# Twenty ring rows, and dots that read the tokens from PSUM

## The reference, cut to what matters

```python
for l in range(DEPTH):                         # 2
    h = _rms(x, g_mix_norm[l])
    x = x + _mixer_block(h, ...)               # w_in (1024 -> 2816), four mixers, w_out
    h = _rms(x, g_ffn_norm[l])
    x = x + _peer(h, w_peer_q[l], peer_sub_keys[l], peer_u[l], peer_v[l])

# _peer, for each chunk of 128 tokens
q = (xc @ w_q).reshape(C, PEER_HEADS, 2, PEER_HALF)          # 8 heads
s = einsum('thpd,hpkd->thpk', q, sub_keys)                   # 128 keys twice
sv, si = top_k(s, 16); cand = all 16 x 16 sums of the two; top, pos = top_k(cand, 16)
eidx = index of the chosen pair (one of 16384); g = softmax(top)
a = einsum('thkd,td->thk', u_tab[eidx], xc)                  # a dot per token and chosen expert
w = g * gelu(a)
return einsum('thk,thkd->td', w, v_tab[eidx])                # weighted sum of the v rows
```

## Time and profile before

| | us |
|---|---|
| three executions | 3384.54, 3361.59, 3390.99 |
| median | 3384.54 |
| profiled execution, first to last instruction (span) | 3383.4 |
| PE busy | 2560.1 |
| DVE busy | 2327.2 |
| POOL busy | 2291.7 |
| ACT busy | 690.9 |
| mean of DMA over the span | 356 GB/s, 1205.57 MB |

### The profile page before, as it was taken

The page is one execution under the profiler, slowest core; times in us unless marked ns, Lnnn a source line. Parts: engine busy times, 40 slices in busy tenths (PEclk is TensorE's granted clock), DMA queues, the critical chain, the costliest instruction groups (busy, mean ns, idle before and its releaser), DMA issues.

```text
span 3383.4 us, 27538 instructions
## 1 busy us (share of the span) xinstructions
PE 2560.1 (76%) x7696; PEld 1422.5 (42%) x7696; DVE 2327.2 (69%) x5442; ACT 690.9 (20%) x1655; POOL 2291.7 (68%) x2052
## 2 busy tenths in 40 slices
PE   6568777986777778877787787987787778666667
PEld 5545344743443435533353443643354334222222
DVE  2495678568689875666668886666668888655554
ACT  2112212123311111112211221123322122101011
POOL 0156766566667676676776777677777777777776
PEclk9789888988888888998899998998899899888888
DMA  5489999998899999998999999999999999999998
GB/s 235 174 320 406 358 377 371 343 378 310 308 376 367 347 344 407 401 379 332 352 394 369 379 373 348 390 397 344 348 358 397 363 382 368 368 367 359 366 366 336
DMA packets 316375, 1205.57 MB, mean 356 GB/s; under 512 B 37184, under 2 KB 37440, under 8 KB 301248
## 3 DMA queue, kind: packets, MB, share of 16 engines
q0 software_dynamic: 294912, 1073.87, 83.9%
q1 hardware_dynamic: 21312, 129.94, 9.7%
HBM read 1201.57 MB, written 2.10 MB: 356 GB/s over the span
## 4 chain that ended last, share of the span: by engine, by line
PE 30%; POOL 22%; issue 18%; DVE 17%; DMA 7%; ACT 3%; another core or an unknown queue 2%; SPq 0%; DVEq 0%; ACTq 0%; POOLq 0%
POOL ring L479 22%; PE psY L815 15%; PE psP L694 8%; DMA ring<-in_v,idx 6%; DVE ring L1067 5%; PE psP L689 4%; DVE x L1076 1%; DMA ring<-in_u,idx 1%; DVE sc L860 1%; PE psT L675 1%; ACT diag L656 1%; DVE hot L1031 1%; DVE hot L1032 1%; DVE pick L1033 1%
## 5 line engine op out<-in xcount | busy, mean ns | idle before, releaser
L815 PE MATMUL psY<-ring,diag 128*128 128x512 f32 x3120 | 1689.6, 685 | 678.0 <-DMA ring<-in_v,idx 270.3
L479 POOL DMA_INDIRECT ring<-in_u,idx x1024 | 1148.1, 1121 | 588.1 <-issue 304.3
L1067 DVE CUSTOM_DVE_ANT_0 ring<-ring,htok 128x1024 f32<-128x1024 f32 x1024 | 1232.4, 1223 | 450.5 <-DMA ring<-in_u,idx 396.5
L479 POOL DMA_INDIRECT ring<-in_v,idx x1024 | 1143.3, 1117 | 490.2 <-issue 284.2
L815 PEld LDWEIGHTS psY<-ring,diag 128*128 128x128 f32 x3120 | 636.9, 216 | 1545.9 <-issue 1087.1
L656 ACT ACTIVATE diag<-cst,wgt 128x128 f32<-128x128 f32 x780 | 275.5, 393 | 480.8 <-PE psY L815 184.9
L1076 DVE SCALAR_TENSOR_TENSOR x<-ring,wgt,x 128x1024 f32<-128x1024 f32 x244 | 313.6, 1285 | 39.5 <-DMA ring<-in_v,idx 27.6
L694 PE MATMUL psP<-wr,hT 128*128 128x256 f32 x1392 | 312.7, 383 | 5.1 <-DMA wr<-in_w_out 3.0
L689 PE MATMUL psP<-hT,wr 128*128 128x256 f32 (+1 forms) x1664 | 314.8, 350 | 0.7 <-ACT hT L517 0.7
L689 PEld LDWEIGHTS psP<-hT,wr 128*128 128x128 f32 x1664 | 282.2, 200 | 49.7 <-issue 23.1
L694 PEld LDWEIGHTS psP<-wr,hT 128*128 128x128 f32 x1392 | 267.6, 193 | 65.4 <-issue 22.9
(11 more groups left out here) (125 smaller groups left out, 1652.3 us busy)
## 6 DMA issues: line engine op xcount, KB each, us to landing
wr<-in_w_in SPq DMA_DIRECT2D x44, 1024.0 KB
wr<-in_w_q SPq DMA_DIRECT2D x40, 1024.0 KB
wr<-in_w_out SPq DMA_DIRECT2D x19, 1024.0 KB
ring<-in_u,idx POOLq DMA_INDIRECT x1024
ring<-in_v,idx POOLq DMA_INDIRECT x1024
ring<-in_w_in SPq DMA_DIRECT2D x11, 1024.0 KB, 13.2
x<-in_x SPq DMA_DIRECT2D x4, 512.0 KB, 20.1
sub<-in_subkeys SPq DMA_DIRECT2D x2, 1024.0 KB
```

Source lines behind the costliest of these rows:

```text
L479: pool.indirect_dma_start(out=ring[:, q % NB], out_offset=None, in_=table, in_offset=bass.IndirectOffsetOnAxis(ap=idx[:, s % NS, n:n + 1], ...
L815: last = nc.tensor.matmul(psY[:, b * 512:(b + 1) * 512], diag[:, m % ND], r[:, b * 512:(b + 1) * 512], start=first, stop=final)
L1067: v.tensor_tensor_reduce(out=r, in0=r, in1=htok[:, s % NS], scale=1.0, scalar=0.0, op0=ALU.mult, op1=ALU.add, accum_out=adot[:, n:n + 1]). ...
```

## The change

- `NB` is 20. `W_EARLY` is 15 (input and output pieces of group 0), in ten places of two rows.
- `psH`, two banks, holds the normed tokens of the current chunk. `place_h` (ACT) copies them there from `htok` once the dots of the chunk before are done, ahead of the gelu of that chunk's last head; the dots read `psH` in place of `htok`. `adot` keeps two heads.
- To free two banks, `psP` and `psT` have one each. Odd pieces go to `psO`, even ones to `psP` (`piece_bank`). Of the wide transposes (hT1, qk, catT, hT2) the first four go to `psT`, the other four to `psS` (`batch_bank`, `wide_transposes`); dil T and conv use `psT` alone (`wait_pst`). `pso_free_for` and `pss_free` wait for the user before.
- To free memory for eight rows, buffers of the mixers and of the search are shared: `stick` lies in `tmq` (q and k pieces), `sub` in `prob` and `probT`, `gain_f` in `cat`, `qT` in `qdT`/`qsT`, `sc` in `later`, `sc2`, `cand` and `hot` in `fm`. New waits guard them (`tops_before`, `uses_before`).
- `sub` and `gain_f` are therefore loaded for each group (`top_parameters`), on SP behind the group's piece 13 (group 0: behind piece 16).

The diff, cut to its core; the renaming of `psP[:, G % 2]` to `piece_bank(G)`, of `psT[:, b % 2]` to `batch_bank(b)` and of `tm` to `tmq` and `tms` is left out.

```diff
-NB = 12
-W_EARLY = 12
+NB = 20
+W_EARLY = N_IN + N_OUT
...
+GROUP_LIST = [steps for steps, *_ in GROUPS]
...
-PSS_LIST = list(numbers("pe", "scores", "logits", "key scores"))
+WIDE = ("hT1", "qk", "catT", "hT2")
+PSS_LIST = list(numbers("pe", "scores", "logits", "key scores", *WIDE))
+PSO_USERS = [k for k in numbers("pe", "dil out", "sgu", "sums", "stick out", "piece")
+             if (k[0] != "dil out" or k[2] == 0) and (k[0] != "piece" or PIECE_NO[k[1], k[2]] % 2)]
...
+        qdsT = sb("qdsT", [P, 2, 2, 2, P])
+        qdT, qsT = qdsT[:, 0], qdsT[:, 1]
...
+        probs = sb("probs", [P, 2, 2, SEQ])
+        prob, probT = probs[:, 0], probs[:, 1]
...
+        stick = tmq[:].rearrange("p j a (b w) -> p (j a b w)", w=MW).rearrange("p (c w) -> p c w", w=SEQ)
+        sub = probs[:].rearrange("p a b (c w) -> p (a b c) w", w=P)
+        gain_f = cat[:].rearrange("p a w -> p (a w)")
+        qT = qdsT[:].rearrange("p a j b t -> p (a j b t)").rearrange("p (n b t) -> p n b t", n=2, b=2)
+        sc = later[:].rearrange("p (n b w) -> p n b w", n=2, b=2)
+        fm_flat = fm[:].rearrange("p a b j t -> p (a b j t)")
+        sc2 = fm_flat[:, 0:2 * P]
+        cand = fm_flat[:, 2 * P:4 * P].rearrange("p (a b) -> p a b", b=TOPK)
+        hot = fm_flat[:, 4 * P:8 * P].rearrange("p (n a b) -> p n a b", n=2, b=TOPK)
...
-        adot = sb("adot", [P, SLOTS])
+        adot = sb("adot", [P, 2, TOPK])
...
         psY = ps("psY", [P, D])
-        psP = ps("psP", [P, 2, 512])
-        psT = ps("psT", [P, 2, 512])
+        psH = ps("psH", [P, D])
+        psP = ps("psP", [P, 512])
+        psT = ps("psT", [P, 512])
...
+        def tops_before(s):
+
+            return PH * GROUP_OF[s][0]
...
+        def piece_bank(G):
+
+            return psO if G % 2 else psP
+
+        def batch_bank(b):
+
+            return psT if b in IN_PST else psS
+
+        def pso_free_for(part, s, i):
+
+            n = PSO_USERS.index((part, s, i))
+            if n == 0:
+                return None
+            before = PSO_USERS[n - 1]
+            if before[0] == "piece":
+                return psp_freed(PIECE_NO[before[1:]])
+            return pso_free, PSO_NO[before] + 1
...
             part, s, i = PSS_LIST[n - 1]
+            if part in WIDE:
+                return tp_taken, BATCH_NO[part, s, i] + 2
...
-                sp.dma_start(gain_f[:], g_ffn[l].partition_broadcast(P)).then_inc(s_late, 16)
-                sp.dma_start(sub[:], subkeys[l]).then_inc(s_late, 16)
+
+            def top_parameters(s):
+
+                last = GROUP_OF[s][-1]
+                sp.wait_ge(normed, NORMED_NO["cat", last] + 1)
+                sp.dma_start(gain_f, g_ffn[s // NC].partition_broadcast(P)).then_inc(gain_in, 16)
+                sp.wait_ge(sticked, uses_before(last + 1))
+                sp.dma_start(sub, subkeys[s // NC]).then_inc(sub_in, 16)
...
                 sp.dma_start(place, src).then_inc(there, 16)
+                if i == (N_IN + 2 if s else N_IN + N_OUT + 1):
+                    top_parameters(s)
...
+            def place_h(s):
+
+                act.wait_ge(normed, NORMED_NO["norm2", s] + 1)
+                if s:
+                    act.wait_ge(dotted, SLOTS * s)
+                nc.scalar.activation(psH[:], htok[:, s % NS], ACT.Copy).then_inc(h_placed, 1)
...
+            place_h(0)
             for J in range(HEADS + 1):
...
                     act.wait_ge(dotted, TOPK * (J + 1))
                     if J:
                         act.wait_ge(w_ready, J)
-                    nc.scalar.activation(gl[:], adot[:, J % PH * TOPK:(J % PH + 1) * TOPK],
+                    if (J + 1) % PH == 0 and J + 1 < HEADS:
+                        place_h((J + 1) // PH)
+                    nc.scalar.activation(gl[:], adot[:, J % 2],
                                          ACT.Gelu_apprx_tanh).then_inc(a_gelu, 1)
...
+            def wait_pst(b):
+
+                n = IN_PST.index(b)
+                if n:
+                    pe.wait_ge(tp_taken, IN_PST[n - 1] + 1)
+
+            def wide_transposes(part, s):
+
+                b = BATCH_NO[part, s, 0]
+                wait_pst(b)
+                transposes(b, [hn[:, k * P:(k + 1) * P] for k in range(4)])
+                wait_for(pe, pss_free(part, s, 0))
+                transposes(b + 1, [hn[:, k * P:(k + 1) * P] for k in range(4, 8)])
...
-                if G >= 2:
+                if G % 2:
+                    wait_for(pe, pso_free_for("piece", s, i))
+                elif G:
                     pe.wait_ge(*psp_freed(G - 2))
...
                     if J < HEADS:
-                        n = h * TOPK + k
+                        if h * TOPK + k == 0:
+                            dve.wait_ge(h_placed, s + 1)
                         landed(dve, ("u", J, k))
                         r = ring[:, at[("u", J, k)] % NB]
-                        v.tensor_tensor_reduce(out=r, in0=r, in1=htok[:, s % NS], scale=1.0, scalar=0.0,
-                                               op0=ALU.mult, op1=ALU.add, accum_out=adot[:, n:n + 1]).then_inc(dotted, 1)
+                        v.tensor_tensor_reduce(out=r, in0=r, in1=psH[:], scale=1.0, scalar=0.0,
+                                               op0=ALU.mult, op1=ALU.add, accum_out=adot[:, J % 2, k:k + 1]).then_inc(dotted, 1)
```

More of the change, by code:

```diff
@@ L169 @@
     k for k in numbers("pe", "dil out", "sgu", "sums", "stick out") if k[0] != "dil out" or k[2] == 0)}
[L170 removed]
+WIDE = ("hT1", "qk", "catT", "hT2")
+PSS_LIST = list(numbers("pe", "scores", "logits", "key scores", *WIDE))
+PSO_USERS = [k for k in numbers("pe", "dil out", "sgu", "sums", "stick out", "piece")
+             if (k[0] != "dil out" or k[2] == 0) and (k[0] != "piece" or PIECE_NO[k[1], k[2]] % 2)]
 HN_LIST = [(part, s) for part, s, _ in numbers("dve", "norm1", "qk", "sgu in", "cat", "norm2")]
[L172 to L173 removed]
+BATCH_NO, _batches, IN_PST = {}, 0, []
+for _part, _s, _i in numbers("pe", "dil T", "conv", *WIDE):
     BATCH_NO[_part, _s, _i] = _batches
[L175 removed]
+    IN_PST.append(_batches)
+    _batches += 2 if _part in WIDE else 1
 def vector_rows(J):
@@ L558, in front @@
                     act.wait_ge(*psp_freed(PIECE_NO[GROUP_OF[s][0], 3]))
-                    nc.scalar.activation(sq[:], tm[:, j, 0:4].rearrange("p a b -> p (a b)"), ACT.Square).then_inc(qk_squared, 1)
+                    nc.scalar.activation(sq[:], tmq[:, j].rearrange("p a b -> p (a b)"), ACT.Square).then_inc(qk_squared, 1)
                 elif part == "qk taken":
+                    if s == GROUP_OF[s][0] and s:
+                        act.wait_ge(s_scores, tops_before(s))
                     for m, (dq, dk) in enumerate(((qdT, kdT), (qsT, ksT))):
@@ L725, in pso_wait @@
             def pso_wait(part, s, i):
-                if PSO_NO[part, s, i]:
-                    pe.wait_ge(pso_free, PSO_NO[part, s, i])
+                wait_for(pe, pso_free_for(part, s, i))
             def front(s, part, i):
@@ L734, in front @@
                     pe.wait_ge(normed, n + 1)
-                    for b in range(2):
-                        transposes(BATCH_NO[part, s, 0] + b, [hn[:, (4 * b + k) * P:(4 * b + k + 1) * P] for k in range(4)])
+                    wide_transposes(part, s)
                 elif part == "piece":
@@ L743, in front @@
                     pe.wait_ge(qk_done, s + 1)
-                    for b in range(2):
-                        transposes(BATCH_NO["qk", s, 0] + b, [hn[:, (4 * b + k) * P:(4 * b + k + 1) * P] for k in range(4)])
+                    wide_transposes("qk", s)
                 elif part == "scores":
@@ L782, in front @@
                     for h in range(H):
-                        last = nc.tensor.matmul(psO[:, h * HD:(h + 1) * HD], sgw[:, h], tm[:, j, 5, h * HD:(h + 1) * HD],
+                        last = nc.tensor.matmul(psO[:, h * HD:(h + 1) * HD], sgw[:, h], tms[:, j, 1, h * HD:(h + 1) * HD],
                                                 start=True, stop=True)
@@ L787, in front @@
                     pe.wait_ge(conv_done, s + 1)
+                    wait_pst(BATCH_NO["conv", s, 0])
                     transposes(BATCH_NO["conv", s, 0], [cv[:, 0], cv[:, 1]])
@@ L918, in front @@
                         dve.wait_ge(cat_squared, s)
+                        dve.wait_ge(normed, NORMED_NO["norm2" if s == GROUP_OF[s][0] else "cat", s - 1] + 1)
                     v.tensor_tensor(cat[:, 1].rearrange("p (h d) -> p h d", d=HD),
@@ L1004, in front @@
                         dve.wait_ge(dotted, SLOTS * (s - NS + 1))
-                    link(v.scalar_tensor_tensor(out=htok[:, s % NS], in0=x[:, c], scalar=rs[:, 0:1], in1=gain_f[:],
+                    if s == GROUP_OF[s][0]:
+                        dve.wait_ge(gain_in, 16 * (GROUP_LIST.index(GROUP_OF[s]) + 1))
+                    link(v.scalar_tensor_tensor(out=htok[:, s % NS], in0=x[:, c], scalar=rs[:, 0:1], in1=gain_f,
                                                 op0=ALU.mult, op1=ALU.mult))
```

84 lines of the change are left out of this document (44 added, 40 removed).

## The result

The changed kernel took 3455.6 us (median of four, 3451.2 to 3457.9), beside 3373.7 us for the kernel before on the same chip (four, 3361.6 to 3391.0): ratio 1.023, interval 1.019 to 1.027. It is slower, where 3225 us was forecast.

The account below looks back on a forecast made before the run. POOL's issue was taken to bound the last stage, row waits the middle ones, the engines' fixed-order chain the first. Stages -185, start -5, costs 11 + 10 + 5 + 4 made -160 from 3383.4: 3225 us, range 3110 to 3340.

Parts of the forecast that it names:

- The reading of POOL: Dots with two SBUF operands hold up POOL's gathers; reading psH frees 290 us, POOL's mean near 0.98 instead of 1.12.
- Rival C: Rows help but the PSUM-operand dot still holds POOL: 1.41 us a gather, -95 instead of -185, about 3315 us; chance 0.13.
- DMA's ceiling: Gathers can run at 410 GB/s, 1.28 us each; the last stage's 368 GB/s is not a full queue.
- rival A: DMA is full already at the last stage's 368 GB/s, so the time stays at 3385 us; chance 0.08.
- the new time is at least: Each stage: at least its bytes over 410 GB/s and its time without DVE's waits for rows; stages sum to -185 us.
- -30 for 151:1223: First stage, heads 0 to 19: DVE's 26 us of row waits go, plus a few more; range 0 to -90 us.
- The term of -45: Last stage, 2894:3361, only gathers: from 467 to 422 us as POOL and DMA both allow; range 0 to -48.
- The restructuring's terms (11 + 10 + 5 + 4 - 5 = 25): Parameter loads per group 11 us, stall at piece 14 10, place_h copies 5, shared banks and buffers 4, earlier start -5.
- rival D: With rows in hand the engines' chain in 151:1223 loosens too, DMA near 410 GB/s: about 3130 us; chance 0.16.
- Rival B: Front chain lengthens beyond the rows' cover: 80 us at piece 14, 94 us of transpose handovers, 3463 us; chance 0.08.
- 10 were forecast: Stall of PE and DVE at w_out piece 14, queued behind 1.5 MB of parameters: +10 us, range 0 to +80.

Follow-up runs that it names:

- s1: Changed kernel with a one-column memset behind each linked step of DVE's front, which the next step waits for: 3252.9 us, 0.996 of the kernel before.
- s2: Kernel before with the same memsets behind each linked step of DVE's front: 3342.4 us, 1.024 of the kernel before without them.
- q1: Kernel before, unchanged, run for its trace on a fast chip: 3255.7 us (one run; the others on this chip 3269.3).
- q2: Changed kernel, unaltered, traced on the same fast chip: 3183.2 us, 0.975 of the kernel before.
- q3: Changed kernel with a group's gain_f and sub loaded behind its piece 14 on SP's queue, not ahead of it, fast chip: 3177.9 us, 0.973 of the kernel before.
- t1: Changed kernel, unaltered (20 rows), again on a slow chip: 3432.2 us, 1.023 of the kernel before.
- t2: Changed kernel with 12 ring rows instead of 20, dots still from PSUM, on a slow chip: 3428.8 us, 1.023 of the kernel before.

## Why the prediction was wrong

**The reading of POOL was right.** The dots with a PSUM operand free it. Its mean fell to 1.01 us on the slow chip and 1.00 to 1.01 on the fast one (1.11 and 1.09 before), where 0.98 was forecast: 224 us of 290. The dots kept 1.22 us (1217 ns, 1223 before), and the 65 ns more on PSUM by the Trainium skill (Perfetto Trace Analysis, "Optimizing Scalar/DVE Operations") showed nowhere. Rival C did not happen.

**DMA's ceiling was right.** On fast chips 409 and 410 GB/s hold over whole stages, so rival A, the rule of 358 GB/s (Trainium skill, DMA: Bandwidth & Descriptors, "Specifications"), falls with a long stretch and not only a window of 10 us. On the slow chip no stage reached it, though slices of 86 us did (412 and 411 GB/s in the page above).

**The step that failed** is, by stage, that "the new time is at least" the time without DVE's waits for rows, which I then used as the new time itself, and with it the -30 for 151:1223. It took the front's chain as fixed, bound by the order in the program. On the slow chip that chain is itself made longer by late signals, and the change comes with more lateness (166 us before, 425 after): heads 0 to 19 +41 us instead of -30, 31 to 36 +23 instead of -8, 47 to 53 +14 instead of -24, 37 to 46 +3 instead of -40, 20 to 30 -6 instead of -38. Nothing in my working allowed a stage with front work to become longer through the parts that I called gains. In the trace of before the lateness was to be seen, and the prediction does not speak of it: "remote" waits of 1.5 to 2.5 us inside a search, where DVE waits for its own step, as in this group.

```profile
L868 DVE MATCH_VALUE_LOAD si<-sv,sc 128x8 f32 x128 | 9.3, 73 | 3.6 <-remote 2.5 <-DVE sv L865 1.1
```

That the front's chain gets longer is shown by the stages; that late signals are what makes it longer rests on the counts above and on s1 and s2, and why the change has more of them is open.

**The last stage was sized by the slow chip.** I put its 46.7 us a head (46.1 over heads 54 to 62) down to POOL's issue at 1.41 us a gather. That POOL paces this stage holds: on a fast chip (q1) it is either busy, 287.6 us, or in a gap before a gather, 88.7 us, for the whole 376. But the size of the hold-up there belonged to the chip. On the fast chip the same kernel with the same dots takes 0.99 us a gather in this stage instead of 1.08, thus 1.29 with the gap, 41.8 us a head, at 405 GB/s, and little is left above DMA's 1.28. The term of -45 was -20 on the slow chip (415 to 395 for nine heads) and -5 on the fast one. Why the same dots hold POOL up less there is not shown.

**On fast chips the sum was too large by about a factor of two.** Forecast -160, measured -79 to -87 against the median of before; by the traces q1 and q2 (73 us apart, as q1 was a quick execution of its kernel):

| heads | forecast | fast chip |
|---|---|---|
| start | -5 | +2 |
| 0 to 19 | -30 | +3 |
| 20 to 30 | -38 | -30 |
| 31 to 36 | -8 | +3 |
| 37 to 46 | -40 | -32 |
| 47 to 53 | -24 | -14 |
| 54 to 62 | -45 | -5 |

The middle stages came as computed from bytes over 410. The restructuring's terms (11 + 10 + 5 + 4 - 5 = 25) measured 12 us. The first stage did not get shorter at all, where -30 was forecast, which disposes of rival D too.

**Rival B had the sign, not the mechanism.** It made the front longer by queues and shared banks. On fast chips all of that and the restructuring's other terms together are 12 us; PE waited for w_out pieces 6.5 us in q2 (3.0 in q1), of which q3 takes away the 4.7 at piece 14, where 10 were forecast. That B's 3463 us lies close to the result is luck. The 8 rows, of which I expected most cover, do not cover late signals: s1 shows that with 20 rows more than half of a delay in DVE's front chain still comes out at the end, and t1 with 20 rows is no faster than t2 with 12.

**What stays open:** why some chips deliver signals late, and whether the freed POOL or the restructuring draws the additional ones. Whether recording itself has a part in it is open too: each timed execution lists its span and granted clock, the profiled one among them, so none is known to have run without being recorded, and the traces that lack 40 to 50% of their records of signals are those of the slow chips.

## What to carry to other kernels

Before a few per cent are put down to a change, run the kernel before on more than one chip: here its own time differed by 3%, and a change of -2.5% turned into +2.3%. In a trace, look first at an engine's waits for its own previous step; here their median was 34 ns, and where some lasted microseconds, the stage table was that chip's as much as the kernel's. Before a wait is called late, find the instruction that it was for, since "issue" can hide a wait for another engine. A DVE operation with both operands in SBUF holds up the gathers that POOL issues meanwhile, and one operand in PSUM ended nearly all of it (1.01 us a gather, 0.94 without hold-up) at no cost in DVE's time; whether the time falls depends on who waits for the rows.

## What the runs showed of the hardware that was not expected

- Two sorts of chips: the same kernel at 3264 to 3269 us and at 3354 to 3374 us, with 0 and 24 late signals of DVE to itself, and 2 and 166 us of lateness in the waits of DVE and ACT. At most five chips were met, and perhaps only one slow one.
- Random rows of 4 KB came at 409 to 410 GB/s for 300 to 440 us on end (q2), with the packet share at 1.02 to 1.03.
- A share of 0.97 to 0.98 beside 366 to 375 GB/s was not a full DMA.
- The 128x1024 copy from SBUF to PSUM took ACT 1.03 us, and one linked step more on DVE costs 0.125 us (59 ns and 66 ns of idle time).
